# The down weights of experts 3 to 31 move to the scalar engine's DMA queue

## The reference, cut to what matters

```python
def expert_rows(args):
    xb, e = args
    h = jax.nn.silu(xb @ w_e_gate[e]) * (xb @ w_e_up[e])   # 1024 -> 512
    return h @ w_e_down[e]                                 # 512 -> 1024
y_rows = lax.map(expert_rows, (x_rows, group_e))
y = segment_sum(y_rows * row_w, row_tok)                   # back to the tokens
```

## Time and profile before

| | |
|---|---|
| median of the runs | 1255.98 us |
| the profiled execution: its time | 1256.03 us |
| its span, first to last instruction | 1254.2 us |
| TensorE busy | 1227.6 us (98%) |
| VectorE busy | 662.0 us (53%) |
| ScalarE busy | 427.0 us (34%) |
| SP's queue (q1) | 278.85 MB |
| ACT's queue (q10) | 2.16 MB |
| mean granted TensorE clock | 0.998 of full |

### The profile page before, as it was taken

One profiled execution on the slowest core, in us unless ns is written; L12 is line 12 of the kernel. 1 busy time (PEld: TensorE's weight loads), 2 busy tenths in 40 slices (PEclk: granted clock), 3 DMA queues, 4 the chain that ended last, 5 costly groups with the idle time before them and its releaser, 6 DMA issues.

```text
span 1254.2 us, 16305 instructions
## 1 busy us (share of the span) xinstructions
PE 1227.6 (98%) x6166; PEld 825.9 (66%) x6166; DVE 662.0 (53%) x970; ACT 427.0 (34%) x619; POOL 60.9 (5%) x68
## 2 busy tenths in 40 slices
PE   9999999999999999999999999999999999999987
PEld 8888888888888888888888886333343334333333
DVE  5497765336365347338434757344454445444447
ACT  5778773223342333333343422211111111111115
POOL 0000000000000000000005200100000000000000
PEclk9999999999999999999999999999999999999999
DMA  7333323362323223222223599999999999999995
GB/s 244 103 93 94 104 63 88 101 174 88 96 68 101 84 67 100 84 84 84 84 67 101 175 401 410 367 412 411 415 415 411 413 415 417 414 417 419 412 422 208
DMA packets 143422, 286.10 MB, mean 228 GB/s; under 512 B 11781, under 2 KB 109173, under 8 KB 118784
## 3 DMA queue, kind: packets, MB, share of 16 engines
q1 hardware_dynamic: 140048, 278.85, 59.7%
q0 software_dynamic: 2544, 4.25, 1.0%
q10 hardware_dynamic: 768, 2.16, 0.4%
HBM read 284.91 MB, written 4.33 MB: 231 GB/s over the span
## 4 chain that ended last, share of the span: by engine, by line
PE 86%; DMA 9%; DVE 3%; ACT 1%; issue 1%; SPq 0%; DVEq 0%; ACTq 0%; POOL 0%; POOLq 0%
PE bank L1568 18%; PE bank L1569 18%; PE bank L1570 18%; PE bank L1905 15%; DMA m_raw<-in_w_e_up_dram 9%; PE bank L1937 7%; PE bank L1961 4%; PE bank L1895 1%; PE bank L1930 1%; DVE wo_lo L918 1%; PE bank L1653 1%; PE bank L1723 1%; PE bank L1597 0%; PE bank L1645 0%; PE bank L1644 0%
## 5 line engine op out<-in xcount | busy, mean ns | idle before, releaser
L1905 PE MATMUL bank<-m_raw,xe 128*64 128x512 f32 x1024 | 233.4, 598 | 12.2 <-DMA m_raw<-in_w_e_up_dram 12.1
L918 DVE TENSOR_TENSOR w_lo<-raw,w_hi 128x1024 fp32r<-128x1024 f32 x120 | 148.1, 1237 | 182.2 <-ACT w_hi L575 180.9
L1568 PE MATMUL bank<-xt_hi,w_hi 128*128 128x512 f32 (+1 forms) x584 | 226.7, 388 | 0.3 <-DVE xt_lo L918 0.3
L1570 PE MATMUL bank<-xt_hi,w_lo 128*128 128x512 f32 (+1 forms) x584 | 225.6, 386 | 0.0
L1569 PE MATMUL bank<-xt_lo,w_hi 128*128 128x512 f32 (+1 forms) x584 | 225.5, 386 | 0.0
L914 DVE TENSOR_TENSOR x<-x,bank 128x1024 f32<-128x1024 f32 x120 | 141.1, 1217 | 100.4 <-PE bank L1961 99.5
L575 ACT ACTIVATE w_hi<-raw 128x1024 fp32r<-128x1024 f32 x120 | 126.1, 1057 | 160.7 <-PE bank L1570 158.3
L1905 PEld LDWEIGHTS bank<-m_raw,xe 128*64 128x64 f32 x1024 | 71.5, 136 | 133.7 <-issue 132.2
L1568 PEld LDWEIGHTS bank<-xt_hi,w_hi 128*128 128x128 f32 x584 | 109.7, 188 | 23.7 <-issue 1.9
L1570 PEld LDWEIGHTS bank<-xt_hi,w_lo 128*128 128x128 f32 x584 | 109.7, 188 | 22.2
L1569 PEld LDWEIGHTS bank<-xt_lo,w_hi 128*128 128x128 f32 x584 | 109.7, 188 | 21.6
(11 more groups left out here) (283 smaller groups left out, 1659.5 us busy)
## 6 DMA issues: line engine op xcount, KB each, us to landing
m_raw<-in_w_e_gate_dram SPq DMA_DIRECT2D x64, 1024.0 KB, 27.0
m_raw<-in_w_e_up_dram SPq DMA_DIRECT2D x64, 1024.0 KB, 27.1
m_raw<-in_w_e_down_dram SPq DMA_DIRECT2D x64, 1024.0 KB, 27.5
raw<-in_w_in_dram SPq DMA_DIRECT2D x88, 512.0 KB, 3.8
raw<-in_w_ret_o_dram SPq DMA_DIRECT2D x16, 512.0 KB, 3.4
raw<-in_w_lru_o_dram SPq DMA_DIRECT2D x16, 384.0 KB, 3.4
raw<-in_w_out_dram SPq DMA_DIRECT2D x8, 512.0 KB, 3.8
x_rows<-in_x_dram SPq DMA_DIRECT2D x4, 512.0 KB, 6.7
```

The costliest lines, as they stand in the source:

```text
L918: return dve.tensor_tensor(dst, a, b_r.bitcast(F32), ALU.subtract)
L1568: pe.matmul(dst, sh, mh, start=first and x == 0, stop=False)
L1570: ins = pe.matmul(dst, sl, mh, start=False, stop=last and x == n - 1)
L1905: last = pe.matmul(bank[side:side + ROWS, 0, :], xe[:, 4 * half + k, :], w[:, FE * k:FE * k + FE], start=half == 0 and k == 0, stop=half = ...
```

## The change

SP issues the down weights of experts 0 to 2 only; those of experts 3 to 31 are issued by ACT, in iteration e of its loop for expert e + 3, behind `xe_out(e + 2)` and ahead of `y_high` of expert e. The slots, the waits on `m_done` and the order in which TensorE uses the units stay as they are.

```diff
             load_gate_up(0)
             for e in range(LAST):
                 load_gate_up(e + 1)
-                load_down(e)
-            load_down(LAST)
+                if e < 3:
+                    load_down(e)
             sp.wait_ge(m_done, M_END - MRING + 4)
...
+            def load_down(e):
+
+                for half in range(2):
+                    n = down_unit(e) + half
+                    act.wait_ge(m_done, n + 1 - MRING)
+                    act.dma_start(m_raw[n % MRING][:, :], w_down[:, ds(e, 1), half:half + 1, :].rearrange("p e h n -> p (e h n)")).then_inc(m_loaded[n % MRING], 16)
+
...
             for e in range(LAST - 1):
                 gate_rows(gu_unit(e + 1), e + 1)
                 xe_out(e + 2)
+                if e + 3 < EXPERTS:
+                    load_down(e + 3)
                 y_high(down_unit(e), 1, y_hi, first_w[:, e:e + 1])
                 ht_out(e + 1, ht)
```

## The result

The changed kernel takes 1273.14 us in the median of four runs (1271.66 to 1274.65), the kernel before 1256.05 us beside it: 17.1 us more, ratio 1.0132 with a 95% interval of 1.012 to 1.0144. The profiled execution took 1274.32 us with a span of 1272.5, 18.3 more than the span before.

The account below looks back on a forecast made before the run. The weight loads were taken as the slower side, the end as unit 187's landing plus 12.4 us of TensorE and the tail. Profiled 1256.0 plus 13.1 for lost order, no rate loss, gave 1269.1 us; range 1264 to 1277.

Parts of the forecast that it names:

- The bound and the order: At the stage's end, down weights overtake gate and up units; unit 181 lands near 1223.1, TensorE then bounds: +13.1 us.
- Taking turns: On the DMA engines, ACT's queue alternates packets with SP's and gets half the bytes; two down units take 9.8 us.
- Rate under two queues: DMA stream from 800 us, both queues active: no loss taken; 2.4% lower rate, +6.6 us, kept for the range.
- My own signs: Right: last weight landing near 1233, down(31) ending near 1249 us; wrong: rate off 416 GB/s by over 1%.
- One line for all queues: ACT's loads are served behind SP's backlog: no change, 1256.0 us, or 1260.9 if only down(30) gets ahead; chance 0.07.
- A faster stream: A second queue fills the stream's holes around the gathers, 12.2 us in all, making up the lost order; chance 0.05.
- ACT held in its issue: SP's full queue holds ACT's issues beyond 5.4 us of slack an iteration: 1376 us, halfway 1296; chance 0.08.

Follow-up runs that it names:

- The runs with one and two experts: The kernel before, with only down weights of expert 31, or of experts 30 and 31, moved to ACT's queue: 1262.38 and 1267.14 us.
- the one on a single queue: The kernel before, all loads on SP, but down weights of experts 30 and 31 issued ahead of expert 31's gate and up weights: 1267.86 us.
- ACT one iteration later, first form: The changed kernel with ACT issuing down weights for expert e + 2 instead of e + 3, SP keeping only experts 0 and 1: 1273.06 us.

## Why the prediction was right, and where its size was off

**The bound and the order.** The prediction said that the end stands at a landing plus TensorE's work, that ACT's queue would get every second packet, and that unit 181 would land with only expert 31's units behind it. In the trace it lands 1239.15 - 1228.28 = 10.9 us before the last landing (10.5 predicted), and from `gate_up(30, 1)` on TensorE needs 13.95 + 12.3 us (13.88 + 12.34 predicted). Of the 18.3 us of the profile 18.3 - 5.5 = 12.8 are this term, against +13.1. The landing of down weights in 10.8 us, the waits of 25.5 us in all and their start near 1000 (the stretch 901 to 1005 has 3.5 us of idle time) are as forecast. The runs with one and two experts and the one on a single queue show that the order does this, not the second queue.

**Taking turns.** The rule of the Trainium skill on the queues ("DMA: Bandwidth & Descriptors", "Queues, rings and completion order") holds with 8 KB packets on both sides as it did for the stores: the two units of down(31) landed at 1225.86 and 1230.70, one in 4.8 us, twice the 2.45 us of a unit alone. The first needed 9.5 us from its issue, of which only these 4.8 are its share of the stream; I had reckoned with the share alone. It changed little, since the pair still passed the units of expert 31.

**The step that failed** is "Rate under two queues". I took no loss and kept +6.6 us for the range; measured are +5.5 us at the last landing (1239.15 against 1233.65). That the 6.6 came near this is luck: they were sized from a stretch of 4 KB packets without a gather against one with a gather, and the loss measured is at the gathers. For the forecast the lower end was chosen with the argument that like packets differ in nothing. That argument holds for SP's and ACT's packets (1213.02 and 1213.07 without gathers), but overlooks the third queue. With that bound the sum would have been 1275.7; the median is 1273.1. My own signs told of it too: the rate is 411 GB/s, off 416 by over 1%, and the last landing and the end of down(31) are at 1239 and 1255, not near 1233 and 1249. Of the 5.5 us about 3.2 are the mean rate (414 to 411 GB/s over 434 us). The last unit's completions on the DMA engines spread over 10.0 us instead of 8.2; that most of the rest lies there is an estimate of mine, no run separates it.

**What was left out.** No step of mine had TensorE's clock. In the changed kernel three half steps behind waits took 5.35 us, one of them at 1164.18 (granted clock 0.72 from 1164 to 1170); all lie ahead of later waits, which absorbed them. In the runs with one expert and with one queue such a step stood at the end and cost 0.8 and 1.9 us.

**The rivals.** One line for all queues: excluded by landings of 10.8 against 39 us. A faster stream: excluded by 411 against 414. But it had a true core that I put the wrong way: 20.6 us of the stream lay at the gathers, and it was not another queue for the weights but half as many, wider gathers that won 9.1 of them. ACT held in its issue: excluded by 0.82 us. The Trainium skill's sentence that issuing from several engines saves only issuing time ("DMA: Bandwidth & Descriptors", "Issuing engines are not separate DMA queues") holds for bandwidth, as without gathers the two kernels' last weights land within 0.05 us of each other; the trace adds that it costs the order between the loads.

## What to carry to other kernels

Where a stream of loads sets the time, one queue in the order of use is a schedule, and a second queue overrules it: whatever is issued there passes all that waits in the first. Look at what lands last and at how much work stands behind it; bytes that were hidden behind the last dependent step cost their full time when they move ahead of it. And before splitting the large loads over queues, take the small transfers beside them away once: here 31 gathers of 4 MB in all held up 201 MB by 20 us.

## What the runs showed of the hardware

- A long issue of SP's doesn't hold ACT's: 0.82 us for two within one of SP's of 4.10 us.
- TensorE's granted clock fell in the longest wait for weights and stayed low in the work behind: 0.69 in an idle stretch of 10 us, 0.71 in the next 7 us, and 16 matmuls took 5.67 instead of 3.65 us. Behind shorter waits it was not regular: 5.21 us behind one of 4.79 and 5.35 behind one of 2.24 (ACT one iteration later, first form), but 3.65 behind those of 3.44 and 3.35 us. There it could fall when the wait was already over. In the changed kernel, with the wait before 1164.18 in the first line:

```profile
1161.90:1164.10 2.20, 0.00 (x0) 0.00 (x0) 1.92 (x2) 0.00 (x0) 0.00 (x0) 1.00 1.00 421
1164.20:1165.00 0.80, 0.80 (x4) 0.35 (x6) 0.00 (x0) 0.00 (x0) 0.00 (x0) 1.00 1.04 440
1165.20:1168.40 3.20, 3.20 (x10) 1.05 (x8) 0.00 (x0) 0.00 (x0) 0.00 (x0) 0.50 1.03 435
```

- An indirect gather of 64 partitions beside a full load stream costs 20.6/31 = 0.67 us of the stream, about 0.3 of it for its bytes (4.25 MB in all at 426 GB/s are 10 us). With 128 partitions the same rows cost little more than their bytes. The rest is time of the weights' own packets. SP's queue from 797 to 1205 us (packets, MB, share of 16 engines' time), in the kernel before, without gathers and with gathers of 128 partitions:

```profile
q1 hardware_dynamic: 22634, 164.84, 98.1%
q1 hardware_dynamic: 23830, 173.55, 100.8%
q1 hardware_dynamic: 23255, 169.36, 98.5%
```

```profile
q0 software_dynamic: 10, 0.04, 66.2%
```

Why the weights' packets are slower beside them is open; no run here gathers 128 partitions as often as 31 times, which would tell the width of a gather from the number of gathers.
